# Ranking all eight experts and holding the first weight transfer until the ids are known

## The chip, the cores and the metric

The kernel runs on one core of one Trainium2 chip. The metric is the device time of one execution in microseconds; the time before is the median of three runs.

## The reference

The kernel computes a two-layer encoder trunk for 256 tokens of width 1024, all in float32. Layer 0 has two parallel attention groups and a dense SwiGLU. Layer 1 has latent attention and then a mixture of experts, which is where the change lies:

```python
def moe_swiglu(h, w_router, w_gu, w_down):
    logits = (h @ w_router).astype(jnp.float32)
    vals, idx = lax.top_k(logits, TOP_K)                 # TOP_K = 2 of 8 experts
    gates = jax.nn.softmax(vals, axis=-1)
    combine = jnp.sum(jax.nn.one_hot(idx, N_EXPERTS) * gates[..., None], axis=-2)
    y = jnp.zeros_like(h)
    for e in range(N_EXPERTS):
        y = y + combine[..., e:e + 1] * swiglu(h, w_gu[e], w_down[e])
    return y
```

Each expert has a gate-and-up matrix of 1024 x 7168 and a down matrix of 3584 x 1024. On the reference's inputs the router sends 51, 91, 66, 30, 87, 61, 55 and 71 tokens to experts 0 to 7 (worked out from the reference, not from a profile).

## The kernel before, in words

Every engine has its own program, and semaphores order them. The dense weights come through a ring of six 1 MB places (`load`, L416). The expert weights come through fifteen 1 MB "homes" (`fill`, L424), which take over the same memory once the dense pieces are done with it. All these transfers are issued by one queue, SyncE's, in program order.

An expert is read as 42 pieces (`EXP`, L102; `NU` = 42). Four of them are issued as two half-size transfers. TensorE takes the pieces in this order: for each, it waits for `home_loaded`, multiplies, and raises `used` (L1950). SyncE waits for `used` of the piece that lay in a home 15 pieces earlier before it refills that home (L480). Homes 0 to 14 are first filled as soon as the dense work frees them (`first_free`, L454): home 0 after the dense SwiGLU, homes 1 to 12 while the last dense pieces are split and used, homes 13 and 14 when the router product is done (`routed`).

The experts stand at eight positions. `GROUPS_AT` (L109) says how many groups of 32 token slots a position has: 3 (96 slots) or 2 (64 slots). TensorE's work for a piece is proportional to that number: four matrix products of 32 rows per group and piece. Position 0 always holds expert 0, so that its transfers need no ids. The other seven experts are ranked on VectorE by their number of tokens (L1443 to L1464), and `RANK_AT` (L110) says which rank stands at which position. The ids go to SyncE as integers (`order_ready`, L1465); SyncE waits for them before the second expert (L473) and loads each with `expert_at` (L465).

Between router and experts, the order on VectorE is: gates, slot numbers, the one-hot slots of position 0 (`mark_slots(0, 1)`, L1440), the ranking, the ids, the overflow flag, the sorted slots and gates of the other positions, their one-hots. TensorE gathers the tokens of position 0 with the first of these one-hots (L1976), ScalarE copies them (L898), and the first expert's products start.

If an expert has more tokens than its position has slots, two further passes over all eight experts run (L505, L1986). They do not in the profile below.

Of the kernel before, what the change touches and what calls it, by code (L numbers as in the profile page):

```python
# [15 lines left out]
P = 128  # L16
D = 1024
SEQ = 256
NT = SEQ // P
# [14 lines left out]
NE, FFE = 8, 3584  # L34
# [71 lines left out]
NG = 3  # L106
CAP = NG * GROUP

GROUPS_AT = (3, 2, 3, 3, 2, 3, 3, 2)  # L109
RANK_AT = (4, 0, 1, 5, 2, 3, 6)  # L110
PASSES = 3
assert len(UQ) == SLOTS and NU % LOOP_HOMES == 0
assert min(GROUPS_AT[0], NG) * GROUP + (PASSES - 1) * CAP >= SEQ
# [78 lines left out]
def build(nc, A):  # L192
# [3 lines left out]
    with ctx:  # L196
# [49 lines left out]
        ones = arena1[:, 2 * P:3 * P]  # L246
        tie = arena1[:, 384:448].rearrange("p (e f) -> p e f", e=NE)
        caps = arena1[:, 448:456]
        rank_at = arena1[:, 457:464]
        names = arena1[:, 465:472]  # L250
        rt = arena1[:, 512:1024]
        onehot_gated = arena1[:, 1024:1024 + NT * NE * CAP].rearrange("p (t e s) -> p t e s", t=NT, e=NE)
        aT_pair = arena1[:, 2560:3072].rearrange("p (j n) -> p j n", j=4)
# [160 lines left out]
        @block.sync  # L414
        def _(sp):
            def load(u, src, n):  # L416
                if u >= RING:

                    sp.wait_ge(lo_ready, u - RING + 1)
                c = src.shape[1]  # L420
                dst = ring[:, u % RING, 0:n].rearrange("p (c n) -> p c n", c=c)
                sp.dma_start(dst, src).then_inc(ring_loaded[u % RING], 16)

            def fill(q, n, e):  # L424
                kind, k, c = EXP[n]
                dst, there = homes[:, HOME_OF[q], :], home_loaded[q]
                if kind == "d":
                    sp.dma_start(dst, expert_source(e, EXP[n])).then_inc(there, 16)
                elif k < SETS:
                    sp.dma_start(dst.rearrange("p (h n) -> p h n", h=2), expert_source(e, EXP[n])).then_inc(there, 16)  # L430
                else:
                    for j in range(2):
                        sp.dma_start(dst[:, j * 1024:(j + 1) * 1024].rearrange("p (h n) -> p h n", h=2),  # L433
                                     expert_source(e, (kind, k, 2 * c + j))).then_inc(there, 16)

            for t in range(NT):
                sp.dma_start(x[:, t, :], A["x"][0, t * P:(t + 1) * P, :]).then_inc(x_loaded[t], 16)
            sp.dma_start(gain, A["l0_norm_attn"].partition_broadcast(P)).then_inc(gain0_loaded, 16)
            sp.dma_start(ident[:, :], A["ident"]).then_inc(ident_loaded, 16)
            for u, piece in enumerate(STREAM):  # L440
                if u == SLOTS:

                    for k, name in enumerate(("l0_a_q_norm", "l0_a_k_norm", "l0_b_q_norm", "l0_b_k_norm")):
                        sp.dma_start(raw_gains[:, k, :], A[name].partition_broadcast(P)).then_inc(tab_in, 16)
                    for t in range(NT):
                        sp.dma_start(rope[:, t, :], A["rope"][t * P:(t + 1) * P, :]).then_inc(tab_in, 16)
                    sp.dma_start(arena3[:, D + 256:D + 512],
                                A["l0_a_lambda"].rearrange("k d -> (k d)").partition_broadcast(P)).then_inc(tab_in, 16)
                    sp.dma_start(subln[:, :], A["l0_a_subln"].partition_broadcast(P)).then_inc(early_loaded, 16)
                    sp.dma_start(sinks[:, 0, :], A["l0_b_sinks"].partition_broadcast(P)).then_inc(early_loaded, 16)  # L450
                    sp.dma_start(rw[:, :, :], A["l1_router"].rearrange("(c p) e -> p c e", p=P)).then_inc(early_loaded, 16)
                load(u, piece_source(piece), piece_floats(piece))

            def first_free(i):  # L454

                if i == 0:
                    sp.wait_ge(used, first(FFN) + len(FFN))
                elif i <= RING:
                    sp.wait_ge(lo_ready, U0 - RING + i)
                elif i <= RING + 2 * SLOTS:  # L460
                    sp.wait_ge(used, U0 - SLOTS + (i - RING - 1) // 2 + 1)
                else:
                    sp.wait_ge(routed, 1)

            def expert_at(i):  # L465
                return sp.value_load(ids_i[0:1, i:i + 1], min_val=0, max_val=NE - 1)

            def main_pass():
                e = 0
                for i in range(NE):  # L470
                    if i:
                        if i == 1:
                            sp.wait_ge(order_ready, 1)  # L473
                        e = expert_at(i)
                    for n in range(NU):
                        m = i * NU + n
                        if m < HOMES:
                            first_free(m)
                        else:
                            sp.wait_ge(used, U0 + m - HOMES + 1)  # L480
                        fill(m % HOMES, n, e)

            def more_pass(p):
                for i in range(NE):
                    e = expert_at(i) if i else 0
                    for n in range(NU):
                        m = i * NU + n
                        if m >= LOOP_HOMES:
                            sp.wait_ge(used, U0 + p * NE * NU + m - LOOP_HOMES + 1)
                        fill(m % LOOP_HOMES, n, e)  # L490

            def store(p):

                for q in range(4):
                    t, c = q // 2, slice((q % 2) * COLS, (q % 2 + 1) * COLS)
                    sp.wait_ge(scat_added, scatters_before(p + 1, 0) - 3 + q)
                    sp.dma_start(A["out"][0, t * P:(t + 1) * P, c], x[:, t, c]).then_inc(stored, 16)
                sp.wait_ge(stored, 64 * (p + 1))

            main_pass()  # L500
            store(0)
            sp.wait_ge(flag_ready, 1)
            most = sp.value_load(nmax_i[0:1, 0:1], min_val=0, max_val=SEQ)
            with sp.If(most > 0):
                for p in range(1, PASSES):  # L505
                    more_pass(p)
                    store(p)
# [469 lines left out]
        def _(v):  # L977
            steps = [0]

            def link(ins):  # L980
                steps[0] += 1
                ins.then_inc(dve_step, 1)
                v.wait_ge(dve_step, steps[0])
# [437 lines left out]
                v.tensor_tensor(xs, xs, bank(b), ALU.add).then_inc(scat_added, 1)  # L1421

            sorted_slot, sorted_gates = rt[:, 440:456], rt[:, 456:472]
            ranks, cnt, over, ids = rt[:, 472:479], rt[:, 480:488], rt[:, 488:496], rt[:, 496:504]

            def mark_slots(e0, e1):
                for t in range(NT):
# [6 lines left out]
                    v.tensor_tensor(onehot_gated[:, t, :, :], onehot[:, t, 0:NE, :],  # L1434
                                    bc(sorted_gates[:, 8 * t:8 * t + 8], 2, CAP), ALU.mult).then_inc(onehot_ready, 1)

            slot_te = slot.rearrange("p (t e) -> p t e", t=NT)
            sorted_te = sorted_slot.rearrange("p (t e) -> p t e", t=NT)
            link(v.tensor_copy(sorted_te[:, :, 0:1], slot_te[:, :, 0:1]))
            mark_slots(0, 1)  # L1440


            v.wait_ge(counted, 2)  # L1443
            link(v.tensor_copy(cnt, bank(7)[:, 0:8]))
            M = NE - 1
            more = rt[:, 64:64 + M * M].rearrange("p (e f) -> p e f", e=M)
            same = rt[:, 256:256 + M * M].rearrange("p (e f) -> p e f", e=M)
            my_count, other_count = bc(cnt[:, 1:NE], 2, M), bc(cnt[:, 1:NE], 1, M)
            link(v.tensor_tensor(more, other_count, my_count, ALU.is_gt))
            link(v.tensor_tensor(same, other_count, my_count, ALU.is_equal))  # L1450
            link(v.tensor_tensor(same, same, tie[:, 1:NE, 1:NE], ALU.mult))
            link(v.tensor_tensor(more, more, same, ALU.add))
            link(v.tensor_reduce(ranks, more, AX.X, ALU.add))


            perm = rt[:, 384:384 + M * M].rearrange("p (i e) -> p i e", i=M)
            link(v.tensor_tensor(perm, bc(ranks, 1, M), bc(rank_at, 2, M), ALU.is_equal))
            picked = rt[:, 256:256 + M * M].rearrange("p (i e) -> p i e", i=M)

# [1 line left out]
                link(v.tensor_tensor(picked, perm, bc(src, 1, M), ALU.mult))  # L1461
                link(v.tensor_reduce(dst, picked, AX.X, ALU.add))

            pick(ids[:, 1:NE], names)  # L1464
            v.tensor_copy(ids_i[0:1, 1:NE], ids[0:1, 1:NE]).then_inc(order_ready, 1)  # L1465
            link(v.tensor_copy(over[:, 0:1], cnt[:, 0:1]))
            pick(over[:, 1:NE], cnt[:, 1:NE])
            link(v.tensor_tensor(over, over, caps, ALU.subtract))
            link(v.tensor_reduce(nmax[0:1, :], over[0:1, :], AX.X, ALU.max))
            link(v.tensor_scalar(nmax[0:1, :], nmax[0:1, :], 0.0, None, ALU.max))  # L1470
            v.tensor_copy(nmax_i[0:1, :], nmax[0:1, :]).then_inc(flag_ready, 1)
            link(v.tensor_copy(sorted_gates.rearrange("p (t e) -> p t e", t=NT)[:, :, 0:1], gates3[:, :, 0:1]))
            for t in range(NT):
                pick(sorted_slot[:, 8 * t + 1:8 * t + NE], slot[:, 8 * t + 1:8 * t + NE])
                pick(sorted_gates[:, 8 * t + 1:8 * t + NE], gates[:, 8 * t + 1:8 * t + NE])
            mark_slots(1, NE)
            v.wait_ge(onehot_ready, 4)
            gate_slots()
# [529 lines left out]
def shape_tables():  # L2008

    def rope(dim):  # L2010
# [7 lines left out]
    return {  # L2018
        "ident": np.eye(P), "rope": np.concatenate(rope(HD) + rope(C_ROPE), 1),
        "triu": i[:, None] < i[None, :], "iota": np.broadcast_to(i[None, :], (P, P)), "tie": tie,  # L2020
        "order": np.broadcast_to(np.concatenate([GROUP * np.array(GROUPS_AT), [-1], RANK_AT, [-1], e[1:]]), (P, 3 * NE)),
    }


# [15 lines left out]
```

## Time and profile before

| | us |
|---|---|
| runs shown: median (lowest to highest) | 1351.27 (1348.99 to 1353.41) |
| profiled execution, its own time | 1353.51 |
| its span | 1351.3 |
| TensorE busy (share of the span) | 1276.5 (94%) |
| VectorE busy | 459.7 (34%) |
| ScalarE busy | 325.9 (24%) |
| bytes read from memory | 413.22 MB |

The span goes from the first to the last instruction of the profiled execution; its own time is 2.2 us longer. A share of busy time is a mean over stages with different limits: up to about 480 us the kernel is in attention and dense work, after that in the experts. The granted clock of TensorE is written as a share of 2.4 GHz.

### The profile page before, as it was taken

Reading aid. Unit: us, or ns where it says so; the run is one execution under the profiler, and the core shown is the slowest. Engines: PE = TensorE matmul, PEld = TensorE weight load, DVE = VectorE, ACT = ScalarE, POOL = GpSimd, SP = SyncE. Lnnn points to the kernel's source line nnn. Section 1 sums busy time; section 2 is a strip of 40 time slices with the busy share of each in tenths; the row PEclk is TensorE's granted clock in tenths of the full one; section 3 lists DMA queues with packets and bytes.
Section 4 is the critical chain, followed back from the end, with each engine's and each line's share of the span. In section 5 each row is a group of like instructions: output and inputs, shape, how many; then the busy total and the mean of one; then the engine's idle time right before and its main releaser. Section 6 shows DMA issues by size and latency. Waiting matters only on the chain.

```text
span 1351.3 us, 22124 instructions
## 1 busy us (share of the span) xinstructions
PE 1276.5 (94%) x9650; PEld 644.3 (48%) x9650; DVE 459.7 (34%) x679; ACT 325.9 (24%) x568; POOL 64.9 (5%) x116
## 2 busy tenths in 40 slices
PE   5888899999778889999999999999999999999996
PEld 4666778888667753343333333333333333333332
DVE  4866545555575432122113122112222112212212
ACT  4455344443467201020011020011010011101101
POOL 3310000000450000000000000000000000000000
PEclk8997899999989979999999999999999999999998
DMA  8413345554521759999999999999999999999994
GB/s 301 167 62 110 125 157 188 186 189 151 185 68 56 272 222 361 375 360 411 410 410 413 406 412 412 407 412 391 413 407 409 413 409 408 412 409 408 397 407 194
DMA packets 117191, 415.78 MB, mean 308 GB/s; under 512 B 9168, under 2 KB 13664, under 8 KB 102624
## 3 DMA queue, kind: packets, MB, share of 16 engines
q1 hardware_dynamic: 116384, 412.25, 78.8%
q0 software_dynamic: 704, 2.04, 0.6%
q8 instruction: 78, 1.28, 0.4%
q14 instruction: 25, 0.20, 0.0%
HBM read 413.22 MB, written 1.05 MB: 307 GB/s over the span
## 4 chain that ended last, share of the span: by engine, by line
PE 85%; DVE 5%; ACT 2%; SPq 2%; DMA 2%; issue 2%; POOL 2%; POOLq 0%; DVEq 0%; ACTq 0%
PE PS L1938 36%; PE PS L1946 18%; PE PS L1556 6%; PE PS L1557 6%; PE PS L1558 6%; PE PS L1864 2%; PE PS L1872 2%; PE PS L1907 2%; PE PS L1664 2%; DMA homes<-in_l_exp_w_down 1%; SPq L433 1%; ACT arena L675 1%; PE PS L1622 1%; DMA arena<-in_l_a_lambda 1%; POOL stat L527 1%
## 5 line engine op out<-in xcount | busy, mean ns | idle before, releaser
L1938 PE MATMUL PS<-homes,tabs 128*32 128x512 f32 x4704 | 515.8, 593 | 0.6 <-ACT tabs L898 0.6
L1938 PEld LDWEIGHTS PS<-homes,tabs 128*32 128x32 f32 x4704 | 149.4, 110 | 340.6 <-issue 336.4
L1946 PE MATMUL PS<-homes,arena 128*32 128x512 f32 x2352 | 258.9, 593 | 1.0 <-DMA homes<-in_l_exp_w_down 0.6
L1490 DVE SCALAR_TENSOR_TENSOR arena<-arena,PS 64x512 f32<-64x512 f32 x63 | 42.8, 680 | 448.9 <-ACT arena L929 448.5
L988 DVE TENSOR_TENSOR w_lo<-ring,w_hi 128x2048 fp32r<-128x2048 f32 (+2 forms) x56 | 123.8, 2219 | 105.3 <-ACT w_hi L624 94.6
L1946 PEld LDWEIGHTS PS<-homes,arena 128*32 128x32 f32 x2352 | 75.3, 110 | 173.7 <-issue 168.6
L1556 PE MATMUL PS<-w_hi,hT_hi 128*128 128x512 f32 (+2 forms) x372 | 144.3, 388 | 13.7 <-DVE w_lo L988 9.8
L1557 PE MATMUL PS<-w_lo,hT_hi 128*128 128x512 f32 (+2 forms) x372 | 142.1, 382 | 0.0
L1558 PE MATMUL PS<-w_hi,hT_lo 128*128 128x512 f32 (+2 forms) x372 | 142.0, 382 | 0.0
L624 ACT ACTIVATE w_hi<-ring 128x2048 fp32r<-128x2048 f32 (+2 forms) x56 | 103.7, 1857 | 94.6 <-PE PS L1558 94.5
L916 ACT ACTIVATE arena<-PS 128x512 f32<-128x512 f32 (+2 forms) x47 | 23.7, 504 | 413.7 <-PE PS L1907 413.4
L929 ACT ACTIVATE arena<-PS 64x512 f32<-64x512 f32 x63 | 37.2, 590 | 256.8 <-PE PS L1938 256.8
L1556 PEld LDWEIGHTS PS<-w_hi,hT_hi 128*128 128x128 f32 x372 | 72.2, 194 | 29.4 <-DVE w_lo L988 11.6
L1558 PEld LDWEIGHTS PS<-w_hi,hT_lo 128*128 128x128 f32 x372 | 71.9, 193 | 13.0
L1557 PEld LDWEIGHTS PS<-w_lo,hT_hi 128*128 128x128 f32 x372 | 72.2, 194 | 12.2
L1519 DVE TENSOR_TENSOR arena<-arena,PS 32x512 f32<-32x512 f32 x42 | 28.5, 679 | 96.5 <-ACT arena L957 95.4
L1502 DVE TENSOR_TENSOR arena<-arena,PS 64x512 f32<-64x512 f32 x21 | 14.3, 679 | 125.1 <-ACT arena L945 125.1
L1494 DVE SCALAR_TENSOR_TENSOR arena<-arena,PS 64x512 f32<-64x512 f32 x63 | 43.5, 691 | 2.0
L527 POOL TENSOR_TENSOR stat<-stat,neg_half 128x1 f32<-128x1 f32 (+4 forms) x24 | 33.1, 1386 | 151.2 <-DVE stat L1016 144.1
L1907 PEld LDWEIGHTS PS<-ident,arena 128*128 128x128 f32 (+2 forms) x188 | 26.0, 208 | 28.6 <-issue 26.8
L1576 PE MATMUL PS<-ident,h_tok 128*128 128x128 f32 x96 | 17.7, 346 | 19.8 <-DVE h_tok L1034 18.9
L1556 PE MATMUL PS<-w_hi,aT_hi 128*128 128x512 f32 x88 | 34.3, 390 | 0.9 <-DVE aT_lo L1004 0.9
(200 smaller groups left out, 898.7 us busy)
## 6 DMA issues: line engine op xcount, KB each, us to landing
homes<-in_l_exp_w_gu SPq DMA_DIRECT2D x192, 1024.0 KB, 15.0
homes<-in_l_exp_w_down SPq DMA_DIRECT2D x112, 1024.0 KB, 15.3
homes<-in_l_exp_w_gu SPq DMA_DIRECT2D x64, 512.0 KB, 11.9
ring<-in_l_ffn_w_gu SPq DMA_DIRECT2D x22, 1024.0 KB, 5.1
ring<-in_l_ffn_w_down SPq DMA_DIRECT2D x11, 1024.0 KB, 4.9
ring<-in_l_w_in SPq DMA_DIRECT2D x9, 1024.0 KB, 11.4
ring<-in_l_w_out SPq DMA_DIRECT2D x4, 1024.0 KB, 5.1
ring<-in_l_c_w_out SPq DMA_DIRECT2D x4, 1024.0 KB, 5.3
```

Of the source, the lines that this page charges most:

```text
L527: pool.tensor_tensor(s, s, neg_half[:, 0:R_COLS[r]], ALU.pow).then_inc(rstd_ready, 1)
L624: a.activation(w_hi[:, u % SLOTS, 0:n], ring[:, u % RING, 0:n], ACT.Copy).then_inc(hi_ready, 1)
L929: a.activation(gate[0:64, g, :], PS[0:64, g, :], ACT.Tanh, scale=0.5).then_inc(gate_ready, 1)
L988: v.tensor_tensor(w_lo[:, u % SLOTS, 0:n], ring[:, u % RING, 0:n], w_hi[:, u % SLOTS, 0:n].bitcast(f32), ALU.subtract).then_inc(lo_ready, 1)
L1490: v.scalar_tensor_tensor(out=act_of[g], in0=gate[0:64, g, :], scalar=1.0, in1=PS[0:64, g, :], op0=ALU.add, op1=ALU.mult).then_inc(half_sil ...
L1494: v.scalar_tensor_tensor(out=act_of[g - 1], in0=act_of[g - 1], scalar=0.5, in1=PS[64:P, g - 1, :], op0=ALU.mult, op1=ALU.mult)\
L1556: pe.matmul(out, xh, wh, start=start, stop=False)
L1557: pe.matmul(out, xh, wl, start=False, stop=False)
L1558: return pe.matmul(out, xl, wh, start=False, stop=stop)
L1907: ins = pe.transpose(bank(b)[:, j * m:(j + 1) * m], cols[:, j % 2, :], ident[0:m, 0:m])
L1938: ins = pe.matmul(PS[GROUP * q:GROUP * (q + 1), g, :], xT[:, cc, g * GROUP:(g + 1) * GROUP], w[:, q * COLS:(q + 1) * COLS], start=c == 0, ...
L1946: ins = pe.matmul(PS[GROUP * q:GROUP * (q + 1), 3 + g, :], tokens_T(k, c, q // 2, g), w[:, q * COLS:(q + 1) * COLS], start=k == 0 and c == ...
```

## The change

All eight experts are ranked, and rank 0 (the fullest) stands at position 0. Positions have 96 and 64 slots in turn: four of 96 and four of 64, where there were five of 96 and three of 64. SyncE waits for `order_ready` before its first expert transfer, and every position's id is loaded. On VectorE the first one-hots come after the ids and after the sorted slots of both token tiles; the tables of the ranking become 8 x 8 instead of 7 x 7.

```diff
-GROUPS_AT = (3, 2, 3, 3, 2, 3, 3, 2)
-RANK_AT = (4, 0, 1, 5, 2, 3, 6)
+GROUPS_AT = (3, 2, 3, 2, 3, 2, 3, 2)
+RANK_AT = (0, 4, 1, 5, 2, 6, 3, 7)
...
             def main_pass():
-                e = 0
+                sp.wait_ge(order_ready, 1)
                 for i in range(NE):
-                    if i:
-                        if i == 1:
-                            sp.wait_ge(order_ready, 1)
-                        e = expert_at(i)
+                    e = expert_at(i)
...
             def more_pass(p):
                 for i in range(NE):
-                    e = expert_at(i) if i else 0
+                    e = expert_at(i)
...
-            slot_te = slot.rearrange("p (t e) -> p t e", t=NT)
             sorted_te = sorted_slot.rearrange("p (t e) -> p t e", t=NT)
-            link(v.tensor_copy(sorted_te[:, :, 0:1], slot_te[:, :, 0:1]))
-            mark_slots(0, 1)
...
-            M = NE - 1
+            M = NE
...
-            my_count, other_count = bc(cnt[:, 1:NE], 2, M), bc(cnt[:, 1:NE], 1, M)
+            my_count, other_count = bc(cnt, 2, M), bc(cnt, 1, M)
...
-            perm = rt[:, 384:384 + M * M].rearrange("p (i e) -> p i e", i=M)
+            perm = tabs[:, 960:960 + M * M].rearrange("p (i e) -> p i e", i=M)
...
-            pick(ids[:, 1:NE], names)
-            v.tensor_copy(ids_i[0:1, 1:NE], ids[0:1, 1:NE]).then_inc(order_ready, 1)
-            link(v.tensor_copy(over[:, 0:1], cnt[:, 0:1]))
-            pick(over[:, 1:NE], cnt[:, 1:NE])
+            pick(ids, names)
+            v.tensor_copy(ids_i[0:1, :], ids[0:1, :]).then_inc(order_ready, 1)
+            for t in range(NT):
+                pick(sorted_slot[:, 8 * t:8 * t + NE], slot[:, 8 * t:8 * t + NE])
+            mark_slots(0, 1)
+            pick(over, cnt)
...
-            link(v.tensor_copy(sorted_gates.rearrange("p (t e) -> p t e", t=NT)[:, :, 0:1], gates3[:, :, 0:1]))
-            for t in range(NT):
-                pick(sorted_slot[:, 8 * t + 1:8 * t + NE], slot[:, 8 * t + 1:8 * t + NE])
-                pick(sorted_gates[:, 8 * t + 1:8 * t + NE], gates[:, 8 * t + 1:8 * t + NE])
+            for t in range(NT):
+                pick(sorted_gates[:, 8 * t:8 * t + NE], gates[:, 8 * t:8 * t + NE])
```

The remaining lines of the diff move the constants of the ranking (`rank_at`, `names`, `ranks`) to rows of eight.

## Rows read from the trace of the kernel before

**Rows 1.** The page's second part: the span in 40 slices of 33.8 us

```profile
PE   5888899999778889999999999999999999999996
DMA  8413345554521759999999999999999999999994
GB/s 301 167 62 110 125 157 188 186 189 151 185 68 56 272 222 361 375 360 411 410 410 413 406 412 412 407 412 391 413 407 409 413 409 408 412 409 408 397 407 194
```

**Rows 2.** Waits of TensorE after 488 us: total, times, longest

```profile
PE PS L1872 <- DVE arena L1519: 2.7, 1, 2.7
PE PS L1946 <- DMA homes<-in_l_exp_w_down: 0.6, 1, 0.6
```

**Rows 3.** Chain of waits: start, us, what (products of the experts: L1938, L1946)

```profile
481.42 6.66 PE PS L1864 x32
488.64 20.81 PE PS L1938 x192
...
607.69 13.73 PE PS L1938 x128
...
690.50 20.60 PE PS L1938 x192
...
811.06 20.60 PE PS L1938 x192
...
1255.52 13.73 PE PS L1938 x128
```

**Rows 4.** Windows: us, busy time by engine, granted clock, DMA share, GB/s

```profile
485.00:488.60 3.60, 3.06 (x17) 2.90 (x16) 3.29 (x11) 0.98 (x2) 0.00 (x0) 0.67 0.00 0
500.00:607.00 107.00, 107.00 (x978) 37.64 (x972) 18.72 (x28) 15.55 (x30) 0.00 (x0) 1.00 0.97 368
811.06:931.60 120.54, 120.54 (x1081) 41.12 (x1076) 24.94 (x38) 14.63 (x27) 0.00 (x0) 1.00 1.01 405
640.00:855.00 215.00, 215.00 (x1916) 73.65 (x1912) 43.37 (x65) 25.25 (x46) 0.00 (x0) 1.00 1.02 410
1022.00:1237.00 215.00, 215.00 (x1920) 71.66 (x1916) 41.68 (x62) 25.49 (x47) 0.00 (x0) 1.00 1.02 410
```

**Rows 5.** The page's sixth part: transfers, KB each, median us to landing

```profile
homes<-in_l_exp_w_gu SPq DMA_DIRECT2D x192, 1024.0 KB, 15.0
homes<-in_l_exp_w_down SPq DMA_DIRECT2D x112, 1024.0 KB, 15.3
homes<-in_l_exp_w_gu SPq DMA_DIRECT2D x64, 512.0 KB, 11.9
```

**Rows 6.** Transfers into the homes issued between 476 and 495 us

```profile
L430 SPq DMA_DIRECT2D homes<-in_l_exp_w_gu x3: 539/540/612, 476.2 to 491.5; - x3
...
DMA to landing us min/median/max: 5.2/5.5/7.2
```

**Rows 7.** Timeline of VectorE: start, us, what, idle before it

```profile
480.93 0.43 DVE L1428 TENSOR_TENSOR arena<-arena 128x96 f32<-128x96 f32 x2
481.28 0.16 DVE L1444 COPY arena<-PS 128x8 f32<-128x8 f32 x1
...
483.42 0.16 DVE L1465 CAST ids_i<-arena 1x7 int32<-1x7 f32 x1
...
484.96 0.21 DVE L1461 TENSOR_TENSOR arena<-arena 128x49 f32<-128x49 f32 x1
...
485.45 0.21 DVE L1461 TENSOR_TENSOR arena<-arena 128x49 f32<-128x49 f32 x1
```

**Rows 8.** Timeline of TensorE: the last product of the token counts

```profile
480.48 0.57 PE L1851 MATMUL PS<-arena 128*128 128x8 f32 x2
```

**Rows 9.** SyncE's load of a flag into a register: ns, first and last start

```profile
L503 SPq TENSOR_LOAD <-nmax_i x1: 282/282/282, 1348.0 to 1348.0; - x1
...
L503 SPq SEQ_ASSERT  x1: 18/18/18, 1348.5 to 1348.5; - x1
```

**Rows 10.** Timeline at the end: the last piece's weights after its transfer

```profile
1334.25 0.16 PEld L1946 LDWEIGHTS PS<-homes,arena 128*32 128x32 f32 x8 [0.88 <-DMA homes<-in_l_exp_w_down]
...
1335.38 0.59 ACT L957 ACTIVATE arena<-PS 64x512 f32<-64x512 f32 x1 [3.09 <-PE PS L1946]
```

**Rows 11.** Windows of 10 us in which TensorE pauses, and the fastest for transfers

```profile
430.00:440.00 10.00, 7.40 (x60) 6.54 (x59) 6.85 (x8) 7.43 (x12) 0.53 (x1) 1.00 0.65 214
460.00:470.00 10.00, 6.99 (x36) 5.83 (x35) 6.01 (x9) 4.41 (x8) 1.12 (x2) 0.85 1.02 409
750.00:760.00 10.00, 10.00 (x92) 3.60 (x88) 0.00 (x0) 0.98 (x2) 0.00 (x0) 1.00 1.03 422
```

More of the change, by code:

```diff
@@ L248, in build @@
         caps = arena1[:, 448:456]
-        rank_at = arena1[:, 457:464]
-        names = arena1[:, 465:472]
+        rank_at = arena1[:, 456:464]
+        names = arena1[:, 464:472]
         rt = arena1[:, 512:1024]
@@ L1423, in _ @@
             sorted_slot, sorted_gates = rt[:, 440:456], rt[:, 456:472]
-            ranks, cnt, over, ids = rt[:, 472:479], rt[:, 480:488], rt[:, 488:496], rt[:, 496:504]
+            ranks, cnt, over, ids = rt[:, 472:480], rt[:, 480:488], rt[:, 488:496], rt[:, 496:504]
             def mark_slots(e0, e1):
@@ L1435, in gate_slots @@
                                     bc(sorted_gates[:, 8 * t:8 * t + 8], 2, CAP), ALU.mult).then_inc(onehot_ready, 1)
-            slot_te = slot.rearrange("p (t e) -> p t e", t=NT)
             sorted_te = sorted_slot.rearrange("p (t e) -> p t e", t=NT)
-            link(v.tensor_copy(sorted_te[:, :, 0:1], slot_te[:, :, 0:1]))
-            mark_slots(0, 1)
             v.wait_ge(counted, 2)
             link(v.tensor_copy(cnt, bank(7)[:, 0:8]))
-            M = NE - 1
+            M = NE
             more = rt[:, 64:64 + M * M].rearrange("p (e f) -> p e f", e=M)
             same = rt[:, 256:256 + M * M].rearrange("p (e f) -> p e f", e=M)
-            my_count, other_count = bc(cnt[:, 1:NE], 2, M), bc(cnt[:, 1:NE], 1, M)
+            my_count, other_count = bc(cnt, 2, M), bc(cnt, 1, M)
             link(v.tensor_tensor(more, other_count, my_count, ALU.is_gt))
             link(v.tensor_tensor(same, other_count, my_count, ALU.is_equal))
-            link(v.tensor_tensor(same, same, tie[:, 1:NE, 1:NE], ALU.mult))
+            link(v.tensor_tensor(same, same, tie, ALU.mult))
             link(v.tensor_tensor(more, more, same, ALU.add))
             link(v.tensor_reduce(ranks, more, AX.X, ALU.add))
-            perm = rt[:, 384:384 + M * M].rearrange("p (i e) -> p i e", i=M)
+            perm = tabs[:, 960:960 + M * M].rearrange("p (i e) -> p i e", i=M)
             link(v.tensor_tensor(perm, bc(ranks, 1, M), bc(rank_at, 2, M), ALU.is_equal))
@@ L2020, in shape_tables @@
         "triu": i[:, None] < i[None, :], "iota": np.broadcast_to(i[None, :], (P, P)), "tie": tie,
-        "order": np.broadcast_to(np.concatenate([GROUP * np.array(GROUPS_AT), [-1], RANK_AT, [-1], e[1:]]), (P, 3 * NE)),
+        "order": np.broadcast_to(np.concatenate([GROUP * np.array(GROUPS_AT), RANK_AT, e]), (P, 3 * NE)),
     }
```

## The prediction

> **What bounds the kernel now.** I read the slices first. From about 500 us to the end TensorE is at nine tenths or more and so are the transfers, most slices at 406 to 413 GB/s [rows 1]. Two resources run at their limit together, so the question is which one has slack.
>
> The waits of TensorE answer it for the kernel as it stands: after the first expert product it waits 0.6 us for a transfer and 2.7 us at the final scatter, and little else [rows 2]. The chain of waits is TensorE's own work from 488.64 us on [rows 3]. So TensorE sets the time now. From its starts I read the price of a position. A 3-group position takes 811.06 - 690.50 = 120.56 us, the first one 607.69 - 488.64 = 119.05 us, a 2-group position 690.50 - 607.69 = 82.81 us [rows 3]. The last one, which gathers nothing afterwards, runs from 1255.52 to 1335.38 us, 79.9 us [rows 3, 10].
>
> The transfers are close behind. All experts together are 192 + 112 full transfers and 64 halves [rows 5], that is 336 MiB or 352.3 MB, 42 pieces of 1.0486 MB per expert. When no home is missing, the rate is 410 GB/s over two stretches of 215 us, which are two experts long, so that every kind of piece is in them [rows 4]. That is 2.557 us a piece and 107.4 us an expert. A 3-group position is thus 13.1 us slower than its transfers, a 2-group position 24.6 us faster. Where TensorE is the slower, the homes fill up and the rate sags: 368 GB/s in the first position, 405 in the fourth [rows 4].
>
> What lets TensorE be the bound is the lead. By 485 us the first fifteen pieces have landed (from 485 to 488.6 nothing moves) [rows 4], and the sixteenth is issued at 491.5 us, when the first piece has been used [rows 6]. Without that stock the whole 352.3 MB would have to pass after the router.
>
> **The change, part by part.**
>
> *One 3-group position becomes a 2-group position.* TensorE's work falls by 120.56 - 82.81 = 37.75 us [rows 3]. This is what the change removes.
>
> *The ids come first.* The chain on VectorE up to the ids waited behind the two one-hot operations at 480.93 us and then copied the counts at 481.28 [rows 7]. Now it starts as soon as the counts are there: their last product starts at 480.48 and takes 0.57 [rows 8], so about 481.15, a gain of 0.1 us. Nine operations between there and the cast grow from 49 to 64 elements. The 96-element one-hots cost 0.22 each against 0.21, so I take 0.01 us each, 0.1 in all. The cast then still ends at 483.42 + 0.16 = 483.6 us [rows 7]. If the copy had to wait as before, it would be 0.1 later; this is small either way.
>
> *SyncE waits for the ids before its first transfer.* Behind that wait stand all 368 expert transfers; the dense loads are ahead of it in the program and are not touched. A register load takes from 1348.0 to 1348.5 [rows 9], so the first issue is at 483.6 + 0.1 (the signal) + 0.6 = 484.3 us. All fifteen homes are free by then (the router product is done), so the queue issues one after another at 0.54 us apiece [rows 6], faster than 2.557 us and no limit. A transfer of 1 MB issued into a quiet queue lands after 5.2 us at the least [rows 6]: the first piece lands at 489.5 us. If it took the 7.2 us of the slowest of these, everything is 2 us later.
>
> *The gather is later.* In front of the first one-hots now stand the ids and the picks of two rows of slots. A pick is two operations, and two picks take 485.45 - 484.96 = 0.49 us apart, so 1.0 us for two; with the one-hots of the first tile and the second another 0.4 [rows 7]. TensorE may gather at 485.1 instead of 481.42, 3.7 us later. The gather takes 6.66 us [rows 3] (at half clock, as now; the clock in that window is 0.67 [rows 4]), and the first product starts at 488.64 + 3.7 = 492.3 us. Two pieces have landed by then, so this delay is covered by the transfers; without that cover it would cost 3.7 us. The wider picks of gates and one-hots run while the first pieces are multiplied, which takes 20.81 us before their transposes are wanted [rows 3], and cost nothing.
>
> *The sum on either side.* TensorE alone would be done with its last piece at 492.3 + 119.05 + 3 x 82.81 + 3 x 120.56 + 79.9 = 1301.4 us. The transfers need 489.5 + 335 x 2.557 = 1346.1 us until the last of 336 pieces has landed. The transfers are later by 45 us, so they are the bound. By pairs of positions: TensorE falls 13.1 us behind in the 3-group half, makes up 24.6 us in the next, and so waits 11.5 us in every pair, four times 11.5.
>
> Do the homes ever hold the transfers up? At the worst, TensorE is 13.1 + 2.8 us behind, 6 to 7 pieces; eight of the fifteen homes are left for pieces on their way. Now a transfer lands 15.0 us after its issue [rows 5], which is 15.0 / 2.557 = 6 pieces in flight at 410 GB/s. Eight are enough, and I charge nothing. The bound above is the sag of the fourth position: 5 GB/s over 120 us [rows 4], 1.5 us, perhaps once or twice.
>
> From the last landing to the end nothing changes: the weights of the last piece are loaded at 1334.25 us [rows 10], which leaves 1351.3 - 1334.25 = 17.1 us for its products, the adds, the scatter and the stores. So the span becomes 1346.1 + 17.1 = 1363.2 us, against 1351.3: plus 11.9 us. In terms of before: the 37.75 us saved on TensorE come to nothing, and the last landing moves from 1334.2 to 1346.1 because the stock of fifteen pieces (38 us of transfers) is gone, less some 26 us (what remains of the two) in which the homes were full or the start was slow. Added to the median of the runs, 1351.27 + 11.9 = 1363.2 us (the profiled execution's own time, 1353.51, lies 2.2 above that median, and by it the sum would be 1365.4).
>
> The one number that carries this is the rate. In the slices it is 413 at the highest [rows 1], which gives 2.539 us a piece and 6 us less; at 408 it is 4 us more.
>
> The Trainium skill ("DMA: Bandwidth & Descriptors", section "Bandwidth", part on measured transfers) gives 425 GB/s for a long transfer of 16 MB and a fabric ceiling of 435. No stretch here holds 425; the fullest rows have 410, and one window of 10 us has 422 [rows 4, 11]. By the page's 425 the sum would be about 1333 us, an estimate from that page; by the rows it is 1363.
>
> **The rivals.**
>
> *The transfers run faster when the homes never hold them up (other side).* For it: one window of 10 us moved 422 GB/s [rows 11]. At that rate a piece takes 2.485 us, the last lands at 489.5 + 832.5 = 1322 us, and the time is 1339 us. Against it: two stretches of 215 us without want of a home have 410, with the 16 engines' share at 1.02 [rows 4], which is full. The point from which it decides is 1334.2 - 489.5 = 844.7 us for 335 pieces, 416 GB/s: above it the kernel is faster than before. Between 414 and 418 it is no difference.
>
> *The waits lower TensorE's clock.* In a 2-group position TensorE would now work 82.81 of 107.4 us or less, with a pause at every piece. Where it paused before, the granted clock was 1.00 at 7.40 of 10 us busy and 0.85 at 6.99 of 10 [rows 11]. At 0.85 a 2-group position takes 82.81 / 0.85 = 97.4 us, and 107.4 - 13.1 = 94.3 us are there for it; 3.1 us are lost in each of four, and the time is 1376 us. It decides only when the mean clock there is under 82.81 / 94.3 = 0.88. At 1.2 GHz throughout it would be 165.6 us and about 1648 us, but then TensorE has no pauses, and in stretches without pauses the clock is 1.00 [rows 4]. The Trainium skill ("TensorE: Matmul & The Clock Gate", section "HAM oscillation — how this bites in real kernels") describes just such waits for a transfer after each block of products as the cause of a clock that falls again and again; its waits are longer than the 0.3 to 0.8 us a piece here.
>
> *The change brings further passes.* With ranks 0 to 3 at the positions of 96 slots (91, 87, 71 and 66 tokens) and 61, 55, 51 and 30 at those of 64, every expert fits. If that were wrong, 16 more positions of 120.56 us would make it 3292 us.
>
> *TensorE stays the bound*, as the change's counts alone would suggest: 1301.4 + 17.1 = 1318.5 us. It would need 352.3 MB in 812 us, 434 GB/s, which no row shows.
>
> **How the numbers follow.** The forecast, transfers as the bound near 410 GB/s, has 0.78; its own range is 1357 (413 GB/s) to 1368 us (408, and a sag). Faster transfers have 0.09: a good half of that lies within 0.3% of before, which is 4 us and about what can be told from no change, and the rest is faster. The clock has 0.11, mostly with small amounts. TensorE as the bound and further passes have 0.01 each. So faster by over 0.3% is 0.05, within it 0.07, slower 0.88. The range of 8 in 10 takes in a part of both neighbours: 1355 to 1373 us.
>
> **What would show it.** Right: no transfer into the homes before 484 us; the transfer share at 1.02 and 410 GB/s from about 490 to 1346 us without sags; TensorE waiting for `homes` about 45 us in all, nearly all of it in 2-group positions; the second expert's last product near 703 us instead of 690.5; the last landing near 1346 us. Wrong: a mean rate above 416 GB/s; TensorE waiting for homes less than 20 us; a granted clock under 0.88 in the 2-group positions; or SyncE waiting long for `used` in the 3-group positions.

## Result and profile after

The changed kernel takes 1373.13 us (median of three runs, 1372.78 to 1377.01), 1.0156 times the kernel before (95% interval 1.0129 to 1.0184). In two further sets of five runs it was 1374.15 and 1374.06 us, 1.0144 times before (1.0118 to 1.0171 and 1.0123 to 1.0166). It is slower by 1.4 to 1.6%. The forecast was 1363.2 us, 9.9 us too low; the median lies a hair past the upper end of its range, 1373, and the two further sets about 1 us past it. The profiled execution took 1372.78 us with a span of 1371.0 us; TensorE was busy for 1251.6 us (91%).

The slices of the page, of 34.3 us each, to be held against [rows 1]:

```profile
PE   5888899999878889999799999889999979999985
DMA  8413445554400089999999999999999999999994
GB/s 308 167 47 108 147 160 184 186 189 138 130 6 16 0 331 412 407 412 412 407 413 413 408 410 412 412 408 410 413 403 409 413 404 409 412 407 410 413 401 184
```

From the twelfth slice to the fourteenth, where the early expert transfers were, nearly nothing moves (6, 16, 0 GB/s). From the sixteenth to the last but one the transfers never sag, and TensorE now drops to 7 or 8 tenths in places. The waits of TensorE after 480 us (total, times, longest), beside [rows 2]:

```profile
PE PS L1931 <- DMA homes<-in_l_exp_w_gu: 21.5, 31, 1.6
PE PS L1939 <- DMA homes<-in_l_exp_w_down: 20.2, 34, 1.2
PE PS L1857 <- DVE arena L1425: 3.9, 1, 3.9
PE PS L1865 <- DVE arena L1512: 2.7, 1, 2.7
```

0.6 us of waiting for weights have become 41.7 us. Most of them lie in the 2-group positions, as windows cut roughly by position show (us, busy times, granted clock, transfer share, GB/s), beside [rows 4]:

```profile
491.50:609.10 117.60, 117.60 (x1076) 40.94 (x1080) 18.38 (x27) 15.07 (x29) 0.00 (x0) 1.00 1.02 410
609.10:709.20 100.10, 88.33 (x748) 27.33 (x744) 19.04 (x29) 11.19 (x20) 0.00 (x0) 1.00 1.02 410
709.20:829.70 120.50, 120.50 (x1080) 41.11 (x1076) 24.36 (x37) 14.63 (x27) 0.00 (x0) 1.00 1.02 410
829.70:942.00 112.30, 102.23 (x880) 31.96 (x876) 20.55 (x31) 10.81 (x19) 0.00 (x0) 1.00 1.02 410
```

Each first number pair is a window's place in the span, the first column after it its length. The first and third windows are 3-group positions: TensorE is busy throughout. The second is a 2-group position; the fourth holds one and then 16 us of the next 3-group position, whose products start at 925.84 us. In each of these two TensorE is idle for 10 to 12 us; the rate is 410 GB/s in all four. The other end of the stream is SyncE. From 480 us on, while it issues the expert transfers, it waits once, for the ids (the first row; the 119.7 us of this wait end before its first expert transfer), and never for a home. The second row group is the transfers into the homes, ns at the least, median and most, and their first and last start:

```profile
SPq L466 <- DVE ids_i L1458: 119.7, 1, 119.7
```

```profile
L430 SPq DMA_DIRECT2D homes<-in_l_exp_w_gu x192: 542/2219/10617, 484.4 to 1299.1; - x192
...
DMA to landing us min/median/max: 5.5/18.9/28.0
```

In [rows 6] an issue took 0.54 us; here the median is 2.2 us. SyncE stands at the queue, as the run few_in_flight below shows: there it waits for a landing before each issue, and the issue itself is back at 0.54 us. The start of the expert stage, on VectorE, TensorE and at the weights of the last piece (start, us, what, idle before), beside [rows 7, 3, 10]:

```profile
482.77 0.16 DVE L1458 CAST ids_i<-arena 1x8 int32<-1x8 f32 x1
...
483.86 0.43 DVE L1425 TENSOR_TENSOR arena<-arena 128x96 f32<-128x96 f32 x2
```

```profile
484.34 6.57 PE L1857 MATMUL PS<-arena,h_tok 128*128 128x96 f32 x32 [3.94 <-DVE arena L1425]
491.49 8.79 PE L1931 MATMUL PS<-homes,tabs 128*32 128x512 f32 x80 [0.58 <-ACT tabs L895]
...
1354.01 0.16 PEld L1939 LDWEIGHTS PS<-homes,arena 128*32 128x32 f32 x8 [1.36 <-DMA homes<-in_l_exp_w_down]
```

The ids are cast 0.65 us earlier than before; this execution was 0.65 us ahead already when the router's result came (475.54 against 476.19 us). The last weights are loaded at 1354.01 us instead of 1334.25: 19.76 us, which is the whole difference of the spans (19.7).

### The profile page after: what moved, and what is told of

Read it like the earlier page. It is cut to its first block, busy times and chain, and to the rows that moved or that the text cites. A ratio compares the mean times of both kernels' runs of the same rounds, so it can differ in the third digit from the quotient of the medians.

```text
span 1371.0 us, 21501 instructions
## 1 busy us (share of the span) xinstructions
PE 1251.6 (91%) x9302; PEld 625.6 (46%) x9302; DVE 451.9 (33%) x665; ACT 320.9 (23%) x559; POOL 65.6 (5%) x116
## 4 chain that ended last, share of the span: by engine, by line
PE 54%; SPq 26%; DMA 8%; DVE 5%; issue 3%; ACT 3%; POOL 1%; POOLq 0%; DVEq 0%; ACTq 0%
PE PS L1931 18%; SPq L430 16%; PE PS L1939 7%; DMA homes<-in_l_exp_w_down 7%; PE PS L1549 7%; PE PS L1550 7%; PE PS L1551 6%; SPq L433 6%; SPq L428 5%; PE PS L1857 2%; PE PS L1657 1%; PE PS L1865 1%; ACT arena L672 1%; PE PS L1900 1%; PE PS L1615 1%
## 5 line engine op out<-in xcount | busy, mean ns | idle before, releaser
L1931 PE MATMUL PS<-homes,tabs 128*32 128x512 f32 x4480 | 497.4, 594 | 22.6 <-DMA homes<-in_l_exp_w_gu 21.5
L1931 PEld LDWEIGHTS PS<-homes,tabs 128*32 128x32 f32 x4480 | 138.8, 110 | 356.2 <-issue 298.3
L1939 PE MATMUL PS<-homes,arena 128*32 128x512 f32 x2240 | 252.0, 594 | 20.3 <-DMA homes<-in_l_exp_w_down 20.2
L1483 DVE SCALAR_TENSOR_TENSOR arena<-arena,PS 64x512 f32<-64x512 f32 x60 | 40.8, 680 | 448.3 <-ACT arena L926 447.9
L1939 PEld LDWEIGHTS PS<-homes,arena 128*32 128x32 f32 x2240 | 69.2, 110 | 193.5 <-issue 154.4
L1487 DVE SCALAR_TENSOR_TENSOR arena<-arena,PS 64x512 f32<-64x512 f32 x60 | 41.4, 690 | 1.9
L1857 PE MATMUL PS<-arena,h_tok 128*128 128x96 f32 (+1 forms) x256 | 32.8, 291 | 3.9 <-DVE arena L1425 3.9
L1569 PE MATMUL PS<-ident,h_tok 128*128 128x128 f32 x96 | 17.4, 341 | 19.8 <-DVE h_tok L1031 18.9
## 6 DMA issues: line engine op xcount, KB each, us to landing
homes<-in_l_exp_w_gu SPq DMA_DIRECT2D x192, 1024.0 KB, 19.7
homes<-in_l_exp_w_down SPq DMA_DIRECT2D x112, 1024.0 KB, 18.9
```

The lines of the kernel that those rows point to most:

```text
L1487: v.scalar_tensor_tensor(out=act_of[g - 1], in0=act_of[g - 1], scalar=0.5, in1=PS[64:P, g - 1, :], op0=ALU.mult, op1=ALU.mult)\
L1857: ins = pe.matmul(bank(b)[:, c * n:(c + 1) * n], h[:, t, cc * P:(cc + 1) * P], oh, start=t == 0, stop=t == NT - 1)
L1931: ins = pe.matmul(PS[GROUP * q:GROUP * (q + 1), g, :], xT[:, cc, g * GROUP:(g + 1) * GROUP], w[:, q * COLS:(q + 1) * COLS], start=c == 0, ...
L1939: ins = pe.matmul(PS[GROUP * q:GROUP * (q + 1), 3 + g, :], tokens_T(k, c, q // 2, g), w[:, q * COLS:(q + 1) * COLS], start=k == 0 and c == ...
```

## The experiments

Three numbers of each profiled execution are enough to compare them: the first issue of a transfer into the homes after the ids, the weight load of the last piece, and their difference.

| kernel | median us | against before (95% interval) | first issue | last weights | difference |
|---|---|---|---|---|---|
| changed | 1373.13 | 1.0156 (1.0129 to 1.0184) | 484.4 | 1354.01 | 869.6 |
| changed_again | 1374.15 | 1.0144 (1.0118 to 1.0171) | 486.0 | 1355.53 | 869.5 |
| changed_third | 1374.06 | 1.0144 (1.0123 to 1.0166) | 486.2 | 1355.51 | 869.3 |
| wait_alone | 1375.89 | 1.0162 (1.0145 to 1.0179) | 486.7 | 1356.61 | 869.9 |
| light_tensor | 1374.97 | 1.0151 (1.0130 to 1.0172) | 488.3 | 1355.75 | 867.4 |
| late_gather | 1375.97 | 1.0163 (1.0141 to 1.0184) | 485.6 | 1355.17 | 869.6 |
| few_in_flight | 1373.32 | 1.0147 (1.0125 to 1.0170) | 484.6 | 1354.15 | 869.5 |
| fewer_instructions | 1371.57 | 1.0125 (1.0107 to 1.0143) | 487.8 | 1352.5 (landing) | 864.7 |
| more_instructions | 1439.46 | 1.0633 (1.0611 to 1.0654) | 483.9 | 1418.55 | 934.7 |
| slots_alone | 1342.84 | 0.9926 (0.9909 to 0.9942) | early | 1320.83 | |
| slots_alone_again | 1342.99 | 0.9925 (0.9907 to 0.9943) | early | 1323.70 | |

In the row marked "landing" TensorE came to the last piece after it had landed, so the record of its landing stands there.

**The parts of the change.** First the wait by itself, in the kernel before:

```diff
                 e = 0
+                sp.wait_ge(order_ready, 1)
                 for i in range(NE):
                     if i:
-                        if i == 1:
-                            sp.wait_ge(order_ready, 1)
                         e = expert_at(i)
```

> The kernel before with one edit: SyncE waits for the ids before its first expert transfer; slots, ranks and the order on VectorE stay. Theory T (transfers set the time as soon as the stock of fifteen pieces is gone): the last landing is at 484 + 5.5 + 335 x 2.58 = 1354 us whatever the slots are, so 1371 to 1375 us, as slow as the changed kernel. Rival W (TensorE's chain of 1334.2 - 488.6 us stays the bound and only starts about 2 us later): 1353 to 1356 us.

It came out nearest to theory T: 1375.89 us, 0.9 us above its range and 20 us above that of rival W. With the 3-group position that the change takes away still there, the difference is 869.9 us, as in the changed kernel. The wait alone makes the whole loss, and the saved 3-group position gives nothing back behind it. TensorE's waits for weights here are only 7.4 and 6.5 us:

```profile
PE PS L1937 <- DMA homes<-in_l_exp_w_gu: 7.4, 11, 0.8
PE PS L1945 <- DMA homes<-in_l_exp_w_down: 6.5, 12, 0.7
```

Then the slots by themselves, with expert 0 still fixed and loaded early, but at a position of 64 slots (it gets 51 tokens):

```diff
-GROUPS_AT = (3, 2, 3, 3, 2, 3, 3, 2)
-RANK_AT = (4, 0, 1, 5, 2, 3, 6)
+GROUPS_AT = (2, 3, 2, 3, 3, 2, 3, 2)
+RANK_AT = (0, 4, 1, 2, 5, 3, 6)
```

> The kernel before with expert 0 fixed at position 0 and loaded early as before, but with four positions of 96 and four of 64 slots: 64, 96, 64, 96, 96, 64, 96, 64, expert 0 (51 tokens) in the first of 64. TensorE's work falls by 37.75 us, the stock of fifteen pieces stays. Theory T: 321 pieces pass from 490.4 us on, the last lands at 490.4 + 5.2 + 320 x 2.58 = 1321 us, so 1338 to 1342 us, about 0.9% faster than before. Rival W (the saving on TensorE counts in full): 1314 us. Rival N (the transfers were the bound of before anyway): 1350 us, no change.

> The version with the early transfers kept and the new slots, in five rounds: 0.8 to 1.0% faster than before, 1339 to 1344 us where before has 1351 to 1354.

Both sets are far nearer to theory T than to its rivals, but a little slower than it says: 1342.84 us is 0.8 us above its range, and the gain of 0.75% (1342.99 us) is under the 0.8 to 1.0% expected. The last weights were foreseen at 1321 us and loaded at 1320.83 and 1323.70. This is the version that beats both kernels, by 0.75% against before and 2.3% against the changed one (1342.99 against 1374.06 us in one set). It gains 11 us and not 37.75, because the transfers set its time for a part of the stage:

```profile
PE PS L1946 <- DMA homes<-in_l_exp_w_down: 9.6, 17, 0.7
PE PS L1938 <- DMA homes<-in_l_exp_w_gu: 8.1, 12, 0.8
```

It holds fewer tokens for expert 0 than before: above 64 the further passes would run.

**Is TensorE's work or the gather part of the bound?** The kernel changed_again served as the control of this set:

> The changed kernel itself, on the chip of the next three. Both theories: 1373 us, 1.4 to 1.7% above the kernel before; TensorE waits for homes some 42 us in all.

```diff
-GROUPS_AT = (3, 2, 3, 2, 3, 2, 3, 2)
+GROUPS_AT = (2, 2, 2, 2, 2, 2, 2, 2)
...
-            link(v.tensor_scalar(nmax[0:1, :], nmax[0:1, :], 0.0, None, ALU.max))
+            link(v.tensor_scalar(nmax[0:1, :], nmax[0:1, :], 0.0, None, ALU.mult))
```

> The changed kernel with 64 slots at all eight positions and no further passes (tokens beyond 64 per expert are left out). TensorE's work falls by four times 37.75 us = 151 us. Theory T (transfers set the time, at 2.58 us a piece from 484 us on): no change, 1371 to 1375 us. Rival W (TensorE's work still sets a good part of it, the 3-group positions above all): faster by 20 us or more. A small gain of 1 to 3 us would be the first piece being used sooner.

151 us less of TensorE's work, by the count of groups, changed nothing that can be told (1374.97 against 1374.15). TensorE waits for weights 146.8 us in all instead of the control's 41.5:

```profile
PE PS L1931 <- DMA homes<-in_l_exp_w_gu: 92.0, 146, 2.0
PE PS L1939 <- DMA homes<-in_l_exp_w_down: 54.8, 92, 2.1
```

These are 105.3 us of waits more and not 151. The profile also has TensorE busy for 105.0 us less and not 151 (1147.8 against 1252.8 us). The other 46 us are in how a piece is recorded. Eight pieces of 16 products each, back to back in the changed kernel, take 13.73 us, 1.72 us a piece:

```profile
829.69 13.73 PE PS L1931 x128
```

A piece of 16 products that is followed by a wait is recorded as 1.92 us of work. So 0.2 us of each pause count as work, and light_tensor has 238 such waits.

The difference of light_tensor, 867.4 us, is 2.1 us under the others; its time is no shorter, because its first issue was 2.3 us later than the control's. The smaller difference was not expected, and it became the clue below.

```diff
-            for t in range(NT):
+            for t in 5 * tuple(range(NT)):
                 pick(sorted_slot[:, 8 * t:8 * t + NE], slot[:, 8 * t:8 * t + NE])
```

> The changed kernel with the two picks of the slots done five times, so that the first one-hots and the gather come 4 x 1.0 = 4 us later, the ids and the transfers at the same time. Theory T: the delay is covered, within 1 us of the changed kernel. Rival W (the path ids, one-hots, gather sets the start of everything): 4 us slower.

TensorE waited 8.0 us for the one-hots instead of 3.9, and began the experts 4.1 us later by the difference of these waits. The span from first issue to last weights stayed 869.6 us. The medians differ by 1.8 us, more than the 1 us expected, with intervals that overlap. So the times alone leave some 2 us open; the trace shows the delay covered.

**Why 2.580 us a piece and not 2.557?** The rate in the long windows is 410 GB/s again, yet 335 pieces took 1354.01 - 484.35 - 5.5 = 864.2 us, 2.580 us each. The windows at the end of the changed kernel show what the mean hides (us, busy times, clock, share, GB/s):

```profile
1344.00:1346.00 2.00, 1.44 (x20) 0.26 (x12) 0.08 (x1) 0.00 (x0) 0.00 (x0) 1.00 0.95 397
1346.00:1348.00 2.00, 1.48 (x20) 0.27 (x16) 0.00 (x0) 0.00 (x0) 0.00 (x0) 1.00 0.52 217
1348.00:1350.00 2.00, 2.00 (x18) 0.56 (x18) 0.00 (x0) 0.00 (x0) 0.00 (x0) 1.00 0.53 209
1350.00:1352.00 2.00, 0.80 (x8) 0.48 (x11) 0.00 (x0) 0.38 (x1) 0.00 (x0) 1.00 0.45 188
1352.00:1354.00 2.00, 1.56 (x16) 0.31 (x8) 0.00 (x0) 0.00 (x0) 0.00 (x0) 1.00 0.05 20
```

From 1346 to 1352 us the sixteen DMA engines together are busy for about half: half of them have nothing left. The trace's landing records, sixteen for each transfer, say the same. Of the last piece, eight shares land within 1.2 us of the first one and the other eight 6.0 to 7.8 us after it. A piece counts as landed when all sixteen shares have, so the pieces go at the pace of the slower half. The gap grows along the way: between the first and the last share there are 0.6 us at the first piece, 3.6 at the 75th transfer, 6.6 at the 207th and 7.9 at the 339th. Was it the depth of the queue?

```diff
                             sp.wait_ge(used, U0 + m - HOMES + 1)
+                        if m >= 6:
+                            k = m - 6
+                            sp.wait_ge(home_loaded[k % HOMES], 16 * main_transfers(k // NU, k % NU))
                         fill(m % HOMES, n, e)
```

> The changed kernel, but SyncE issues the transfer of a piece only when the piece six before it has landed completely, so at most six are under way (it was about seven, by a landing time of 18.9 us). Theory S (some of the sixteen DMA engines are slower for good and every piece waits for the slowest, 2.58 us a piece; the faster ones only run ahead): the time is the same, 1371 to 1377 us, and the engines end closer together than the 8 us now. Rival Q (a deep queue lets the engines drift apart and that costs the 8 us): 2.557 us a piece as the mean rate of 410 GB/s says, 1363 to 1366 us. If six are too few to keep the engines busy, the share of the transfers is under 1.00 and the time is higher than 1377.

The time and the difference stayed (1373.32, 869.5 us), so the depth is not the cause. The second half of the expectation failed: the engines did not end closer together. The share falls from 0.97 to 0.62 at 1346 us and to 0.05 only at 1352, as without the limit, and the shares of the last piece still land 7.9 us apart. Six pieces, 15 us, are room enough for 8 us of drift. The run also shows that issuing is no limit: its median issue into the homes took 0.54 us instead of 2.2, at the same time in all.

What else differed in light_tensor was the number of instructions. The page counts 75 packets of 16 KB in the queue that loads them for the changed kernel (57 of them between 480 us and the last weights), and 64 in light_tensor. From here on changed_third is the control.

> The changed kernel again, on the chip of the next three. From the first issue of an expert transfer to the weight load of the last piece 869.6 us, as in its three relatives so far; 1370 to 1376 us.

```diff
+                    thin = p == 0 and ((kind == "gu" and 0 < c < (KC if k < SETS else KC // 2) - 1) or
+                                       (kind == "d" and n < NU - 1 and 0 < c < 3))
-                    for g in range(ng):
+                    for g in range(ng - 1 if thin else 0, ng):
...
-                            for q in range(4):
+                            for q in range(3 if thin else 0, 4):
```

> The changed kernel with 26 of the 42 pieces of each expert multiplied by one product instead of 8 or 12 (the rest of the products is left out); waits, transfers and signals stay. TensorE's expert instructions fall by more than half, and the 16 KB packets of the instruction queue in the expert stage from some 58 to about 27. Theory I (the instruction loads fall on half of the sixteen DMA engines, about 1.07 us each, 58 x 1.07 / 8 = 7.8 us, and every piece waits for the slowest engine): from first issue to last weight load 869.6 - 4.1 = 865.5 us, and the time falls by about 4 us. Rival E (some engines are slower by themselves): 869.6 us, no change. Rival W (TensorE's work matters): far more than 4 us.

The packets fell from 75 to 46 (the pages of changed_third and of this run):

```profile
q8 instruction: 75, 1.23, 0.4%
q8 instruction: 46, 0.75, 0.2%
```

The difference fell from 869.3 to 864.7 us, 4.6 us where theory I had 4.1 and rival E none. The gap between the first and the last share shrank as well, but not by half everywhere: from 6.6 to 4.2 us at the 207th transfer, and from 7.5 to 6.5 us at the last. The median is only 2.5 us lower, with intervals that overlap, so the times do not settle it; the trace does. In the two profiled executions 1.6 us of the 4.6 are hidden by a later first issue, and 1.3 us by a longer stretch from the last weights to the end (18.1 us against 16.8). The run leaves out TensorE's work together with its instructions, so by itself it cannot tell their loading from the products' reading of the homes. The next run adds instructions and leaves the products as they are.

```diff
             rsqrt(R_NORM3 + 1)
+            for _ in range(16000):
+                pool.engine_nop()
```

> The changed kernel with 16000 empty instructions on GpSimd, which has nothing to do in the expert stage; 1 MB of instructions more, some 62 packets. Theory I: if they fall on the same engines, 62 x 1.07 / 8 = 8 us slower (last weight load 878 us after the first issue); if on the other eight, up to no change; if on one engine, up to 60 us. Rival E: no change, whatever the engines.

65 us slower than its control, at the same bytes of weights, where the expectation had up to 60 us if the packets fell on one engine. Its DMA queues (packets, MB, share of sixteen engines) and slices show where:

```profile
q1 hardware_dynamic: 116384, 412.25, 74.8%
q8 instruction: 75, 1.23, 0.3%
q14 instruction: 150, 1.23, 0.2%
```

```profile
GB/s 311 184 4 136 142 177 181 200 166 126 59 6 15 189 410 395 362 384 372 298 410 359 311 399 390 350 310 403 377 293 411 412 404 412 413 406 413 412 407 208
```

125 more instruction packets, 1 MB beside 352 MB of weights, pull the rate down to between 293 and 410 GB/s while they last (to about 1080 us), and then it is 410 again. Rival E, engines slow by themselves, cannot do that. The packets were of 8 KB in another queue than TensorE's, 125 and not 62. The landing records show that they delay one engine and not eight: of the 75th transfer fifteen shares land within 1.1 us, and the sixteenth 14.8 us after the first. From the 21st to the 230th transfer the last share comes 9.9 us (median) after the fifteenth; in changed_third it is 0.1 us. The packets' own time is 41 us in all. Why they cost 65 us stays open, and the trace does not name the engine. The 16000 empty instructions also ran on GpSimd while their packets were loaded; no run has the one without the other.

## Why the prediction was right, and where it was off

- *Which resource bounds.* Right. The stock gone, the transfers set the time; light_tensor and wait_alone show it from both sides. Foreseen were 45 us of waits for weights, measured 41.7, and that they agree is partly luck. The last landing came 7.9 us later than in the sum, which by itself makes 53 us of waits; but 0.2 us of each of the 65 waits, 13 us, stand in the profile as work.
- *The start.* Right: first issue 484.4 us (484.3), gather 484.34 (485.1), first product 491.49 (492.3). The gather's delay is covered.
- *The homes never hold the transfers up.* Right: SyncE never waited for one, and there was no sag. It was closer than foreseen: a transfer landed 18.9 us after its issue and not 15.0, which is seven pieces under way and not six, of the eight homes that the prediction had for them.
- *335 pieces at 2.557 us.* Here the sum was off, and with it the size: the forecast was 11.9 us slower than before, and 21.9 us were measured. It took the rate of the slices, a mean over sixteen engines, for the pace of a piece, which is that of the slowest. At 2.580 us it is 7.9 us more (last weights 1354.01 against 1346.1). The range gave this number 4 us to the slow side; the drift was in the trace of before as well (in its landing records, 0.4 to 6.6 us between the first and last share of a transfer, rising and falling), but there the stream paused whenever TensorE was behind, and the slower engines could catch up.
- *The tail.* Right: 17.0 us from the last weights to the end (17.1).
- *From the span to the runs.* The other 2 us: the profiled execution of before lay 2.2 us above its median and that of after 0.35 below; 0.4 us go the other way, since the time exceeds the span by 1.8 us after and by 2.2 before.
- *The end of the second position.* Foreseen at 703 us, measured 709.15. The gather for the third position stands ahead of the last two pieces; this shifts TensorE within the pair and costs nothing.
- *Rival: faster transfers.* No. The windows have 410 GB/s with a queue that is always full; the 425 GB/s that the Trainium skill gives for a transfer of 16 MB ("DMA: Bandwidth & Descriptors", section "Bandwidth") were not reached over any such window here either.
- *Rival: the clock.* No. In the 2-group windows the granted clock was 1.00 at 88.33 of 100.10 us busy, and in light_tensor 0.99 at 177.65 of 215 us, with 238 waits of 0.6 us in the mean and 2.1 at the most. Such pauses leave the clock at 2.4 GHz all but throughout. The rival is not empty, though: in fewer_instructions, with waits of up to 2.8 us and TensorE busy for 166.18 of the same 215 us, the granted clock was 0.87, so TensorE ran a part of that time at 1.2 GHz. There too the transfers set the time.
- *TensorE as the bound, further passes.* Neither.

## What to carry to other kernels

When two resources are near their limits, write down each one's finishing time from its own first start, stock included: a wait placed ahead of a stream costs the stream's lead, here fifteen pieces, and no saving on the other engine gives it back. Where a transfer spreads over sixteen engines, take its pace from landings and not from the mean rate; here it was one per cent slower. Of a change in two parts, one may be good and be buried by the other: the slots alone were 0.75% faster.

## What the runs showed of the hardware

By these runs, loading instructions takes DMA time from the weights; only the execution of the added instructions was not told apart from it. In a stage in which the sixteen engines' mean share is 1.02, 29 packets of 16 KB fewer (and the products that they hold) shortened 869.3 us to 864.7, and 125 packets of 8 KB of empty instructions for GpSimd lengthened it by 65 us, with one engine's share late. The 57 packets of the changed kernel's expert stage took 1.08 us each. Spread over eight engines that would be 7.7 us on each, an estimate from these two numbers, beside the 7.9 us that the last weights came late. That all of it is theirs, and that they fall on the half of the engines that is late, is inferred and not shown. The Trainium skill ("Runtime: NRT & Kernel Launch", section "Instruction fetch mechanics") calls the cost of crossing a block of instructions mostly hidden; for the engine that executes them the trace agrees (TensorE is busy for 120.50 of 120.50 us in the third window above), but for the transfers beside them it is not hidden.
